# A hybrid decoder step on one Trainium2 core: the second output projection cut into units, half of them between the GLA steps

## The reference

```python
y_c = _merge(_head_norm(o_c, p['gdn_norm_g'], rms=True)) * jax.nn.silu(z_c)   # DeltaNet, 512 rows
y_d = _merge(_head_norm(o_d, p['gla_norm_g'])) * jax.nn.silu(r_d)             # GLA, 512 rows
y = jnp.concatenate([y_c, y_d], -1) @ p['w_out1']                             # 1024 x 1024
x = _layer_norm(ALPHA * x + y, p['ln1_mix_g'], p['ln1_mix_b'])
```

## Time and profile before

| | |
|---|---|
| median of the runs | 1544.57 us |
| profiled execution | 1545.56 us, of which the span is 1543.7 us |
| busy share of the span | PE 92%, DVE 63%, ACT 48%, POOL 15% |
| mean granted TensorE clock | 0.92 of 2.4 GHz |
| instructions | 18458 |

### The profile page before, as it was taken

One profiled execution on the slowest core, in us unless ns is written; L12 is line 12 of the kernel. 1 busy time (PEld: TensorE's weight loads), 2 busy tenths in 40 slices (PEclk: granted clock), 3 DMA queues, 4 the chain that ended last, 5 costly groups with the idle time before them and its releaser, 6 DMA issues.

```text
span 1543.7 us, 18458 instructions
## 1 busy us (share of the span) xinstructions
PE 1423.6 (92%) x7933; PEld 1240.2 (80%) x7933; DVE 977.1 (63%) x939; ACT 744.3 (48%) x622; POOL 231.3 (15%) x166
## 2 busy tenths in 40 slices
PE   7999999799999789998989767999999999999994
PEld 6898886799999578996676666788888888888883
DVE  4533366554553657742535556688988889888886
ACT  4434322432332674321313325577766777677771
POOL 0110303000000000001222030000000002366562
PEclk9999997899999988998556958999999999999998
DMA  6422634645424122211132528799999996400002
GB/s 242 155 96 82 230 96 129 210 123 184 147 83 144 45 69 69 87 55 55 26 118 79 199 87 313 275 377 372 374 391 379 374 372 236 164 28 14 15 14 97
DMA packets 80891, 254.81 MB, mean 165 GB/s; under 512 B 11569, under 2 KB 47701, under 8 KB 68009
## 3 DMA queue, kind: packets, MB, share of 16 engines
q1 hardware_dynamic: 66008, 224.53, 40.3%
q0 software_dynamic: 14800, 29.10, 6.1%
HBM read 306.09 MB, written 16.70 MB: 209 GB/s over the span
## 4 chain that ended last, share of the span: by engine, by line
PE 79%; DVE 7%; DMA 6%; ACT 5%; issue 3%; POOL 0%; POOLq 0%; SPq 0%; DVEq 0%; ACTq 0%
PE PS L612 11%; PE PS L614 10%; PE PS L613 10%; PE PS L1271 7%; PE PS L1273 7%; PE PS L1276 7%; DMA u_raw<-in_w_moe 4%; PE PS L592 3%; PE PS L1294 2%; PE PS L1298 2%; PE PS L1295 2%; PE PS L1008 2%; ACT u_hi L1656 1%; PE PS L677 1%; PE PS L739 1%
## 5 line engine op out<-in xcount | busy, mean ns | idle before, releaser
L2509 DVE TENSOR_TENSOR u_lo<-u_raw,u_hi 128x2816 fp32r<-128x2816 f32 x144 | 442.1, 3089 | 106.2 <-ACT u_hi L1656 105.8
L1656 ACT ACTIVATE u_hi<-u_raw 128x2816 fp32r<-128x2816 f32 x144 | 367.5, 2561 | 181.7 <-DMA u_raw<-in_w_moe 115.5
L612 PE MATMUL PS<-x_in_hi,p_hi 128*128 128x304 f32 x480 | 159.9, 333 | 10.6 <-DVE x_in_lo L1898 10.6
L613 PE MATMUL PS<-x_in_lo,p_hi 128*128 128x304 f32 x480 | 149.6, 312 | 0.0
L614 PE MATMUL PS<-x_in_hi,p_lo 128*128 128x304 f32 x480 | 149.6, 312 | 0.0
L1271 PE MATMUL PS<-u_hi,xg_hi 128*128 128x512 f32 x576 | 142.5, 380 | 5.6 <-DVE xg_lo L2588 3.2
L1273 PE MATMUL PS<-u_hi,xg_lo 128*128 128x512 f32 x576 | 141.3, 377 | 0.0
L1276 PE MATMUL PS<-u_lo,xg_hi 128*128 128x512 f32 x576 | 140.1, 375 | 0.0
L612 PE MATMUL PS<-x_out_hi,w_parts 128*128 128x304 f32 x416 | 128.2, 308 | 8.5 <-DVE x_out_lo L1898 8.5
L614 PE MATMUL PS<-x_out_hi,w_parts 128*128 128x304 f32 x416 | 127.3, 306 | 0.0
L613 PE MATMUL PS<-x_out_lo,w_parts 128*128 128x304 f32 x416 | 126.8, 305 | 0.0
(11 more groups left out here) (545 smaller groups left out, 2527.5 us busy)
## 6 DMA issues: line engine op xcount, KB each, us to landing
u_raw<-in_w_moe SPq DMA_DIRECT2D x96, 1408.0 KB, 8.5
p_raw<-in_w_first SPq DMA_DIRECT2D x40, 512.0 KB, 3.5
p_raw<-in_w_second SPq DMA_DIRECT2D x28, 512.0 KB, 3.5
dring<-in_ffn_w_down SPq DMA_DIRECT2D x8, 1408.0 KB, 7.1
wring<-in_ffn_w_gate SPq DMA_DIRECT2D x9, 1024.0 KB, 5.5
wring<-in_ffn_w_up SPq DMA_DIRECT2D x9, 1024.0 KB, 8.5
wring<-in_w_out SPq DMA_DIRECT2D x2, 2048.0 KB, 7.7
o_rows<-zT POOLq DMA_DIRECT2D x6, 512.0 KB, 6.0
```

Of the source, the lines that this page charges most:

```text
L612: mm(out, w[0], x[0], start=start, stop=False)
L613: mm(out, w[0], x[1], start=False, stop=False)
L1656: A(uhi[n % HIS][:], uraw[n % RAW][:], COPY).then_inc(s("u_hi"), 1)
L2509: TT(ulo[n % RAW][:], uraw[n % RAW][:], uhi[n % HIS][:].bitcast(F32), SUB).then_inc(s("u_lo"), 1)
```

## The change

The output projection of layer 1 becomes eight units of 512 KB, packed behind the input units in one array. Units 0 to 3 multiply DeltaNet's 512 rows (two 128-column tiles a unit, 12 wide matmuls each), units 4 to 7 GLA's. Units 0 and 1 stand between GLA's scores and chunk products, units 2 and 3 between its heads' outputs, with the carried-state matmuls of two heads (two after each three wide ones). DVE adds the first halves to the scaled residual in place (`partial1`). Units 4 to 7 come last, as before after the split of GLA's half. The transposes of GLA's values and their copies move up into the input units 25 and 26; GLA's values, attention and keys move out of `arena` to other buffers; the keys' transposes, DeltaNet's state products and GLA's scores change order and banks.

```diff
 SP
-            for g in range(GEND):
-                group(g)
+                if n % NHALF == 0:
+                    sp.wait_ge(*at(("g_o", "l_qk")[n // NHALF], 4))
+                if n >= NHALF:
+                    sp.wait_ge(*at("b_hi", n - NHALF + 1))
+                sp.dma_start(oraw[n][:], I["w_second"][NU1 + n]).then_inc(s(f"b_ld{n % NHALF}"), 16)
...
             for n in range(RAW):
-                if n == RAW - 1:
-                    sp.wait_ge(*at("b_lo", 4))
+                if n < NHALF:
+                    sp.wait_ge(*at("b_hi", NHALF + n + 1))
                 unit_load(n)
 PE
+            def out1(n, bank, free, between=None):
+                w, x = (ohi[n % 3], olo[n]), xsplit["out"]
+                pe.wait_ge(*at("b_lo", n + 1))
+                for j in range(2):
+                    d = 2 * (n % NHALF) + j
+                    pe.wait_ge(*free(d))
+                    for k in range(4):
+                        kx = k + (4 if n >= NHALF else 0)
+                        last = mm3(PS[:, bank(d), 0:T], [w[0][:, 4 * j + k, :], w[1][:, 4 * j + k, :]], [x[0][:, kx, :], x[1][:, kx, :]], k == 0, k == 3)
...
+                if n == 25:
+                    pe.wait_ge(*at("g_tok_d", 6))
+                    pe.wait_ge(*q_evicted(23))
+                    for i in range(2):
+                        tokens(4 + i, i, 20).then_inc(s("l_vt"), 1)
+                if n == 26:
+                    pe.wait_ge(*at("l_tok", 1))
+                    tokens(4, 2, 20).then_inc(s("l_vt"), 1)
             pe.wait_ge(*at("q_ev", len(REST)))
             pe.wait_ge(*at("sv_ev", len(ORDER)))
-            pe.wait_ge(*at("g_tok_d", 6))
+            pe.wait_ge(*at("l_tok", 3))
...
+            g_state(0)
+            head_vars("g_")
+            pe.wait_ge(*at("l_dqk", 1))
+            for i, (a, n) in enumerate(TILES):
+                if i == 2:
+                    pe.wait_ge(*at("g_rstd", 1))
...
+            pe.wait_ge(*at("g_stu", 1))
+            g_state(1)
+            pe.wait_ge(*at("l_tok", 6))
+            g_state(2)
+            g_state(3)
+            l_scores(0)
+            pe.wait_ge(*at("g_stu", 2))
+            l_scores(1)
+            pe.wait_ge(*at("xlo", 9))
+            first_half(0)
+            pe.wait_ge(*at("g_stu", 3))
+            l_scores(2)
+            l_scores(3)
+            pe.wait_ge(*at("l_vb0", 1))
+            pe.wait_ge(*at("g_stu", 4))
+            pe.wait_ge(*at("l_att", 2))
+            l_chunks(0)
+            first_half(1)
+            pe.wait_ge(*at("l_att", 4))
+            l_chunks(1)
+            pe.wait_ge(*at("ld_stG", 32))
+            pe.wait_ge(*at("l_sc", 2))
+            l_out(0)
+            l_out(1)
+            first_half(2, l_carried(0))
+            l_out(2)
+            l_out(3)
+            first_half(3, l_carried(2))
+            head_means("l_")
+            l_state(0)
+            head_vars("l_")
+            pe.wait_ge(*at("b_ev", 8))
+            l_state(1)
+            pe.wait_ge(*at("l_stu", 1))
+            l_state(2)
+            pe.wait_ge(*at("l_stu", 2))
+            l_state(3)
...
             pe.wait_ge(*at("xlo", 10))
-            group(0, xsplit["out"], lambda t: [at("l_stu", 2)])
-            group(1, xsplit["out"], lambda t: [at("l_stu", 4)], between=mean_between("n1m_", 4 * GEND))
-            ln_sum("n1m_", [6, 7], "b_ev", 4 * GEND)
+            for n in range(NHALF, 2 * NHALF):
+                out1(n, lambda d: OUTB[d], lambda d: OUTF[d])
+                if n == 7:
+                    ln_sum("n1m_", range(4), "b_ev", 16)
+            ln_sum("n1m_", range(4, KT), "b_ev", 16)
 ACT
+                if n == 26:
+                    act.wait_ge(*at("st_conv", 16))
+                    value_tokens(0)
+                    value_tokens(1)
+            value_tokens(2)
...
+            out1_hi(0)
             act.wait_ge(*at("g_var", 1))
...
-            norm("l_", lambda: proj_hi(0))
+            out1_hi(4)
+            norm("l_", lambda: out1_hi(5))
             x_hi("out", 1, mix, at("l_out", 1))
-            act.wait_ge(*at("l_state_pe", 4))
-            proj_hi(1)
-            proj_hi(2)
-            proj_hi(3)
+            out1_hi(6)
+            out1_hi(7)
 DVE
+            l_att(0)
+            l_att(1)
+            out1_lo(2)
+            partial1(0)
+            partial1(1)
+            l_att(2)
+            l_att(3)
+            out1_lo(3)
+            l_chunks(0)
+            partial1(2)
+            partial1(3)
+            l_chunks(1)
+            for d in range(4, KT):
+                partial1(d)
```

More of the change, by code:

```diff
@@ L219, in build @@
         phi = [split(f"p_hi{r}", wring_at + 1024 * (PRAW + r), [128, KT, 128]) for r in range(PHI)]
+        orw_at = [a_at + 1024 * r for r in range(4)] + [wring_at + 4096 + 1024 * r for r in range(4)]
+        ohi_at = [st_at + 6144, st_at + 7168, a_at + 4096]
+        oraw = [nc.alloc_sbuf_tensor_at(f"o_raw{n}", [128, KT, 128], F32, offset=SBUF0 + 4 * at_) for n, at_ in enumerate(orw_at)]
+        olo = [split(f"o_lo{n}", at_, [128, KT, 128]) for n, at_ in enumerate(orw_at)]
+        ohi = [split(f"o_hi{n}", at_, [128, KT, 128]) for n, at_ in enumerate(ohi_at)]
         def unit0_done(n):
             return at("a_pe", n + 1 if n < 32 else 2 * n - 30)
-        def proj_parts(i, part):
-            return wc[:, i % 2, part].rearrange("p (k n) -> p k n", k=KT)
         def gu_parts(j, part):
@@ L556, in _ @@
                 unit1(n)
-            for g in range(GEND):
-                group(g)
+            for n in range(2 * NHALF):
+                out1(n)
             def unit_load(n):
@@ L614, in mm3 @@
                 return mm(out, w[1], x[0], start=False, stop=stop)
[L616 to L630, removed]
             def unit0(n, between=None):
@@ L667, in out_unit @@
                     last.then_inc(s("a_pe"), 1)
+                    if between is not None:
+                        between(4 * j + 3)
+            def out1(n, bank, free, between=None):
[7 more added lines that the diff above has]
+                        last = mm3(PS[:, bank(d), 0:T], [w[0][:, 4 * j + k, :], w[1][:, 4 * j + k, :]], [x[0][:, kx, :], x[1][:, kx, :]], k == 0, k == 3)
+                        if between is not None and k < 3:
+                            between(4 * j + k)
+                    last.then_inc(s("b_pe"), 1)
                     if between is not None:
@@ L1121, in _, with g_state @@
                 last.then_inc(s("g_o"), 1)
[L1122 to L1127, removed]
+            def g_state(h):
                 pe.wait_ge(*at("g_vb", h + 1))
@@ new lines, in _ @@
+            head_vars("g_")
[3 more added lines that the diff above has]
+                    pe.wait_ge(*at("g_rstd", 1))
+                for p in range(2):
+                    last = tr(PS[0:n, (5, 0)[i // 2], 256 * (i % 2) + 128 * p:256 * (i % 2) + 128 * p + 128], k2[:, p, a:a + n], 128)
+            last.then_inc(s("l_kt"), 1)
+            pe.wait_ge(*at("g_stu", 1))
+            g_state(1)
+            pe.wait_ge(*at("l_tok", 6))
@@ L2457, in g_update @@
                 state_update("g_", stA, h, GPAIRS[h], dbc[:, h, 3:11])
-            norm("g_", 0, 12, "gdn", rms=True, prepare=lambda: g_update(0))
-            for h in range(1, H):
-                g_update(h)
+            norm("g_", 0, 12, "gdn", rms=True, prepare=lambda: (g_update(0), out1_lo(0)))
+            g_update(1)
+            x_lo("out", 0, mix, 9)
+            out1_lo(1)
+            g_update(2)
+            g_update(3)
             for h in range(H):
@@ L2495, in l_update @@
                 last.then_inc(s("l_stu"), 1)
-            x_lo("out", 0, mix, 9)
-            norm("l_", 4, 24, "gla", prepare=lambda: (l_update(0), proj_lo(0)))
+            out1_lo(4)
+            dve.wait_ge(*at("st_gp", 16))
+            norm("l_", 4, 24, "gla", prepare=lambda: (l_update(0), out1_lo(5)))
             l_update(1)
@@ L2502, in _ @@
             l_update(3)
-            proj_lo(1)
+            out1_lo(6)
+            out1_lo(7)
             residual1()
```

150 lines of the change are left out of this document (65 added, 85 removed).

## The result

The changed kernel is slower: its median is 1557.4 us against 1543.7 of the kernel before on the same chip, a ratio of 1.0095 (95% interval 1.0071 to 1.0120). The forecast was 1552, a ratio of 1.005. The sign was right, the size about half of what came.

What follows compares the result with a forecast made beforehand. PE was taken as the bound, at half clock in GLA's outputs. Shifts of +18.4 to the outputs' end, +2.0, -15.7 and late MoE weights gave +7.2 us: 1552 against the median, range 1548 to 1557 (1541 to 1558 with rivals, without A).

Steps and rivals of the forecast that it cites:

- Value transposes: Transposes of GLA's values moved into input units 25 and 26, where PE is dense: +0.88 and +0.45 us.
- The third value copy ahead of the decay matmul: Before DeltaNet's outputs: the decay matmul now waits for a 512-column ACT copy, 0.4 to 0.7, taken as +0.5 us.
- From DeltaNet's outputs to the first output: Ahead of GLA's outputs: PE's added work, then DVE's two chunk sums before the first output; +4.5 us, range +2 to +8.
- Outputs with units 2 and 3: GLA's outputs stay at 26.2 us; 48 wide matmuls added on the path at 1.2 GHz cost +12.1 us.
- Rival A: GLA's outputs with units 2 and 3 run at 2.4 GHz: 19.8 instead of 38.3 us, end at 1533.5; chance 0.15.
- Norm's chain: After the head means: chain keeps its length, but the last state product waits for DVE's second update; +2.0 us.
- Last half and MoE weights: Up to ACT's first square: projection's last half at 15.3 us saves 15.7, but late MoE weights delay ACT; net -13.1 us.
- Rival C: Everything ahead of the outputs at 1.2 GHz, +3.5, and second MoE unit landing at 11.7 us, +2.7: 1558; chance 0.10.

Runs made afterwards that it cites:

- both gains: Against the changed kernel: no gap ahead of the outputs, and the first two MoE units' weights loaded early; ratio 0.9913 to the kernel before.
- the last three: Added in turn to no gap with early MoE weights: later wait for third value copy, DeltaNet's second state product during norm wait, unit 4 earlier; ratios 0.9873, 0.9844, 0.9881.
- the best kernel: No gap, early MoE weights, later wait for the third value copy, plus DeltaNet's second state product moved into the wait for its norm; ratio 0.9844 to the kernel before.

## Why the prediction was wrong in size

Faster or slower was called rightly, and what it said the profile would show is there: means at 835.7, the outputs at 0.51, a gap of 3.77 us ahead of the first output, a last half of 15.35 us from 859.7, and ACT's MoE copies released by a DMA. (The profile books the gap as "issue"; that the wait for the running states makes it is shown by the kernel without that wait.) The terms came out so:

- *Value transposes*: +1.23 against +1.33. Right.
- *The third value copy ahead of the decay matmul*, taken at +0.5 and as a wait that costs itself: +2.19. The wait grew by 0.57 (1.08 - 0.51), as priced. The other 1.6 us lie in the products behind it, which ran at 0.50 earlier than before (the fall came 7.4 us after the decay product's start, not 9.2). This was the first term that failed: it held nothing for the clock of the work behind the wait. That the wait moved the fall is not shown, as the three kernels without it have it at 6.4, 14.8 and 14.7.
- *From DeltaNet's outputs to the first output*: +7.03 against +4.5, which is the second. I priced "three DeltaNet states (2.1 for the first, ...)" by the earlier trace rows, where the first ran at the full clock behind a wait of 1.67 us. In the changed kernel the second state product no longer stands ahead of that wait, PE is idle for 3.37 us, and all three run at 0.50: 11.7 us (765.15 to 776.84) in place of the 9.7 of the sum, so +2.0, and the chain stays that much late. The rest is unit 0 (5.5 for 5.2) and the scores and chunk behind it (3.3 for 2.8), less 0.3 up to the first output. With the state product put into that wait, 3.0 to 3.2 us came back there in one kernel and 1.2 to 1.5 in the next, which has the same code up to there.
- *Outputs with units 2 and 3*: +12.35 against +12.1. The size is right and its reason was wrong, so a part of this is luck. I argued that outputs and carried products hold the clock down, from 26.19 of 26.20 us busy at 0.51 in the earlier trace rows, "without any idle time". But that row starts behind the idle time. Two windows of the kernel before, cut where the clock changes, show what the mean of 0.51 hid:

```profile
787.90:791.20 3.30, 1.38 (x11) 1.13 (x9) 2.96 (x10) 0.00 (x0) 0.00 (x0) 1.00 0.99 375
791.30:816.80 25.50, 25.50 (x119) 25.18 (x118) 4.08 (x9) 1.27 (x3) 0.00 (x0) 0.50 0.00 1
```

There too PE came to the outputs at 1.00, waited for the running states (the 1.92 us of the earlier trace rows, which I had called short), and lost the clock some 0.6 us after the first output had begun, as in the changed kernel. The first head shows it: its attention product takes 1.28 us, those of the other three 1.81 each. No run takes this wait out of the kernel before, but the kernel with units 2 and 3 moved out has the same order of outputs without a wait ahead of them, and there they took 20.3 us. Without the gap the interleaved stretch ran at 1.00 throughout. Rival A had its condition right ("the wait for the running states leaves PE idle"), and the kernel that met it was 21 us faster where I gave 18.5.

- *Norm's chain*: +2.73 against +2.0.
- *Last half and MoE weights*: -11.25 against -13.1. The half took its 15.3 us. The second MoE unit landed 4.84 us after the first, where I had taken 2.9 from the earlier trace rows; that is the third failed term, 1.9 us. In the second profile of the same kernel the landings were 3.2 apart, after a later first one, and the sum was the same.

Together 7.0 us are missing, 4.2 of them in the two terms where a wait of PE was priced by its length and the products behind it by rows at the other clock. Rival C had put +3.5 on "everything ahead of the outputs at 1.2 GHz"; its sum of 1558 was the nearest to what came, though unit 1 and the second chunk product ran at 1.00.

The Trainium skill, "TensorE: Matmul & The Clock Gate", Part 1, has the clock follow recent activity and warns that a kernel's point of change moves from run to run. On the second the traces agree: with one and the same code the fall came 6.4 or 14.7 us after the decay product's start. On the first they agree as far as idle time goes: the one wait of 3.75 us, taken out and put back, set the clock of the work behind it. But a PE that the profile shows busy without a break lost the clock too, at 821.2, 808.0, 818.2 and 802.2 us in three kernels.

## What to carry to other kernels

Price a wait of PE by what stands behind it, not by its length: where the next stretch of small products would go on at the full clock, ask whether the wait lets the clock fall first. A row at the half clock tells what work costs at that clock, not that it makes the clock; cut the stretch into fine windows at its entry, and look at the clock there and at the wait just ahead of it, however short. And where wide products are there to be moved, put them between small ones that follow a high clock, as they hold it for their neighbours, rather than into the idle time that looks free.

## What the runs showed of the hardware that I had not expected

- The same matmuls took 38.3 us at a clock of 0.51 or 20.8 at 1.00, by whether PE had stood still for 3.75 us ahead of them. Shorter waits went both ways: 0.71 us ahead of the first chunk product left the clock at 1.00 each time. Through a wait of 1.3 us ahead of GLA's head variances it stayed there in two kernels (no gap, both gains), while in the last three it fell within 1.1 us of the wait's end. In the kernel before it fell behind 1.92 us.
- The clock fell four times in stretches without idle time (near 821, 808, 818 and 802, in three kernels), each time within or right behind a block of carried products that follows two outputs, and among the outputs in none of the five kernels that entered the same products at 1.00 with wide ones between them.
- The same code ahead of DeltaNet's outputs took 49.1, 52.1 and 54.6 us in the profiles of three kernels that share it, as the clock fell early or late in it. That this makes a part of the runs' spread (1508 to 1527 us in the best kernel) is likely but not shown.
